# Updating both triangles of a block inverse by products, instead of one by products and one by transposes

## The reference, cut to what matters

```
m = jnp.where(strict, jnp.einsum('bhnrd,bhnsd->bhnrs', kb, k) * decay, 0.0)
t_mat = m + jnp.eye(c, dtype=m.dtype)
w = lax.linalg.triangular_solve(t_mat, kb * jnp.exp(G)[..., None],
                                left_side=True, lower=True, unit_diagonal=True)
u = lax.linalg.triangular_solve(t_mat, v * beta[..., None],
                                left_side=True, lower=True, unit_diagonal=True)
```

## Time and profile before

| what | value |
|---|---|
| runs before | 1982.77, 1983.9 and 1984.44 us, median 1983.9 us |
| profiled execution | 1982.77 us, its span 1981.0 us |
| PE busy | 1905.2 us, 96% of the span |
| DVE, ACT, POOL busy | 997.3, 749.4, 228.9 us |
| mean granted clock of TensorE | 0.985 |
| share of PE in the chain that ended last | 90% |

### The profile page before, as it was taken

How to read it: one execution, slowest core, us unless ns; L and a number is a source line. 1 busy time by engine, 2 the same in 40 slices (tenths; PEclk the granted TensorE clock), 3 DMA queues, 4 the chain that set the end, 5 groups by cost and what they waited for, 6 DMA issues and landing times.

```text
span 1981.0 us, 25408 instructions
## 1 busy us (share of the span) xinstructions
PE 1905.2 (96%) x8897; PEld 1543.1 (78%) x8897; DVE 997.3 (50%) x1467; ACT 749.4 (38%) x1081; POOL 228.9 (12%) x196
## 2 busy tenths in 40 slices
PE   7989978889999999999999999999999999999998
PEld 6778856567788888888878888888776778888887
DVE  5463478754677774344454444433557443434322
ACT  5542543443544443232233323222455443222322
POOL 0051000012111111100021111110000111111100
PEclk9999989899999999999999999999999999999999
DMA  6310210011333333333333333333321123333332
GB/s 188 86 32 1 54 33 22 22 64 54 95 95 95 95 93 97 97 96 98 101 89 96 95 95 95 92 97 98 91 80 43 33 85 96 97 99 99 89 97 72
DMA packets 309219, 161.23 MB, mean 81 GB/s; under 512 B 12688, under 2 KB 306832, under 8 KB 309024
## 3 DMA queue, kind: packets, MB, share of 16 engines
q1 hardware_dynamic: 308080, 157.64, 27.6%
q0 software_dynamic: 640, 2.17, 0.3%
q10 hardware_dynamic: 432, 0.52, 0.1%
HBM read 158.21 MB, written 2.10 MB: 81 GB/s over the span
## 4 chain that ended last, share of the span: by engine, by line
PE 90%; DVE 5%; ACT 2%; issue 2%; DMA 1%; SPq 0%; POOL 0%; DVEq 0%; ACTq 0%; POOLq 0%
PE ps L365 26%; PE ps L367 26%; PE ps L366 26%; PE ps L1404 1%; PE ps L1019 1%; PE ps L1610 1%; PE ps L1419 1%; PE ps L1031 1%; PE ps L1900 1%; PE ps L1901 1%; PE ps L892 1%; PE ps L1395 1%; PE ps L1601 1%; DMA mx<-in_x 0%; PE ps L1239 0%
## 5 line engine op out<-in xcount | busy, mean ns | idle before, releaser
L365 PE MATMUL ps<-xhi,whi 128*128 128x512 f32 x1656 | 661.5, 399 | 10.1 <-DVE xlo L437 6.7
L366 PE MATMUL ps<-xlo,whi 128*128 128x512 f32 x1656 | 646.2, 390 | 0.0
L367 PE MATMUL ps<-xhi,wlo 128*128 128x512 f32 x1656 | 646.1, 390 | 0.0
L352 ACT ACTIVATE whi<-raw 128x1024 fp32r<-128x1024 f32 (+2 forms) x297 | 308.9, 1040 | 716.1 <-PE ps L367 713.5
L360 DVE TENSOR_TENSOR wlo<-raw,whi 128x1024 fp32r<-128x1024 f32 (+2 forms) x297 | 365.8, 1232 | 281.3 <-ACT whi L352 281.2
L365 PEld LDWEIGHTS ps<-xhi,whi 128*128 128x128 f32 x1656 | 312.0, 188 | 82.3 <-issue 5.4
L367 PEld LDWEIGHTS ps<-xhi,wlo 128*128 128x128 f32 x1656 | 311.8, 188 | 66.0
L366 PEld LDWEIGHTS ps<-xlo,whi 128*128 128x128 f32 x1656 | 312.1, 188 | 65.4 <-issue 3.7
L594 DVE TENSOR_TENSOR zS<-ps,rs 128x512 f32<-128x512 f32 x132 | 91.3, 692 | 293.7 <-PE ps L367 284.6
L367 PE MATMUL ps<-h_hi,wlo 128*128 128x512 f32 x528 | 205.4, 389 | 0.0
L365 PE MATMUL ps<-h_hi,whi 128*128 128x512 f32 x528 | 205.4, 389 | 0.0
(11 more groups left out here) (320 smaller groups left out, 1784.1 us busy)
## 6 DMA issues: line engine op xcount, KB each, us to landing
raw<-in_conv_ffn_w SPq DMA_DIRECT2D x52, 512.0 KB, 3.8
raw<-in_mla_ffn_w SPq DMA_DIRECT2D x52, 512.0 KB, 3.8
raw<-in_w_up SPq DMA_DIRECT2D x44, 512.0 KB, 3.7
raw<-in_w_in SPq DMA_DIRECT2D x28, 512.0 KB, 3.8
raw<-in_conv_w_in SPq DMA_DIRECT2D x24, 512.0 KB, 3.7
raw<-in_w_down SPq DMA_DIRECT2D x16, 448.0 KB, 3.6
raw<-in_conv_ffn_w SPq DMA_DIRECT2D x16, 448.0 KB, 3.6
raw<-in_mla_ffn_w SPq DMA_DIRECT2D x16, 448.0 KB, 3.6
```

The costliest lines, as they stand in the source:

```text
L352: a.activation(whi[:, u % PARTS, 0:n], raw[:, u % RAW, 0:n], ACT.Copy).then_inc(hi_split, 1)
L365: t_.matmul(out, wh, xh, start=first, stop=False)
L366: t_.matmul(out, wh, xl, start=False, stop=False)
L367: return t_.matmul(out, wl, xh, start=False, stop=last)
```

## The change

For the levels below 32 the transposes go. In their place PE makes X O X itself, in the columns of X that change (the first half of each pair), with the same 128 x 64 helper, right ahead of its transpose, head by head. DVE now waits for both results of a head, subtracts the first from `X_` and then the second from `XT_`. The next level's Y waits for the first of these. Level 32 is as it was. `credit` shrinks from 40 columns to 8, which moves all later SBUF tiles down by 128 bytes a partition.

```diff
-        credit = sb("credit", [P, 40])
+        credit = sb("credit", [P, 8])
...
-                    pe.wait_ge(*after(f"gdn X1 {h} taken" if b == 2 else f"gdn X{b // 2} {h} taken"))
+                    pe.wait_ge(*after(f"gdn X1 {h} taken" if b == 2 else f"gdn XOX{b // 2} {h} taken"))
                     pe_block_products(pe, f"gdn Y{b} {h}", mx[:, o_tile(b, h), :], mx[:, X_ + h, :])
                 for h in range(4):
                     pe.wait_ge(*after(f"gdn Y{b} {h} taken"))
                     if b > 2:
                         pe.wait_ge(*after(f"gdn XOXT{b // 2} {h} taken"))
+                    if b < 32:
+                        pe_half_products(pe, f"gdn XOX{b} {h}", mx[:, XT_ + h, :], mx[:, OX + h, :], b, False)
                     pe_half_products(pe, f"gdn XOXT{b} {h}", mx[:, OX + h, :], mx[:, XT_ + h, :], b, True)
-                if b < 32:
-                    for h in range(4):
-                        pe_transpose(pe, f"gdn X{b} {h}", mx[:, XT_ + h, :], f"gdn XOXT{b} {h} taken")
...
                 for h in range(4):
+                    dve.wait_ge(*after(f"gdn XOXT{b} {h} full"))
+                    if b < 32:
+                        x, bank = halves(mx[:, X_ + h, :], b, False), full(dve, f"gdn XOX{b} {h}")[:, 0:T // 2]
+                        v.tensor_tensor(x, x, bank.rearrange("p (n b) -> p n b", b=b), ALU.subtract).then_inc(
+                            *step("dve", f"gdn XOX{b} {h} taken"))
                     x, bank = halves(mx[:, XT_ + h, :], b, True), full(dve, f"gdn XOXT{b} {h}")[:, 0:T // 2]
...
-                if b < 32:
-                    for h in range(4):
-                        v.tensor_copy(halves(mx[:, X_ + h, :], b, False),
-                                      halves(full(dve, f"gdn X{b} {h}"), b, False)).then_inc(
-                                          *step("dve", f"gdn X{b} {h} taken"))
```

## The result

| | before | after |
|---|---|---|
| median | 1983.61 us (4 runs, 1982.77 to 1984.44) | 2002.72 us (4 runs, 2001.36 to 2004.43) |
| ratio | | 1.0097, 95% interval 1.008 to 1.0114 |
| profiled execution, its span | 1982.77, 1981.0 us | 2003.55, 2001.7 us |

The kernel became slower, as forecast, but by 19.1 us and not by 7.1; 2002.7 lies outside the range of 1987.8 to 1994.0. The forecast was wrong in size, and the greater part of the loss is at a place where it had booked nothing.

A forecast was written before the change was run, and what follows sets the result against it. The prediction took PE's issue to bound the kernel: 14.08 us of half products added less 7.00 us of transposes removed, all else 0, took the median from 1983.9 to 1991.0 us, range 1987.8 to 1994.0.

The forecast's parts named there:

- The step that failed: Layout behind credit: later tiles moving by 128 bytes cost 0, since no operand changes shape or stride.
- the half-product batch: 16 added matmuls at each of levels 2 to 16: 3.52 us a level, bounded by 1.75 and 3.57 us.
- What bounds the stage: In the inverse, PE sets the pace: busy 40.60 of 40.60 us, 8.84 us a level.
- The price of a record: On PE in the inverse: an fp32 half product costs two records, 0.220 us, a transpose one, 0.109 us.
- The rival by which 64 columns cost half: In the inverse, half products paid by columns: 1.79 us per 16, +0.2 us in all, 1984.1 us; chance 0.04.
- The sum for the products: Levels 2 to 16: 14.08 us of half products added, 7.00 us of transposes removed, +7.08 us.
- The waits: In the changed levels, added waits stay hidden, cost 0; rival with an exposed wait: 1995.1 us, chance 0.04.
- Absorption: Behind the stage, 0 of the delay absorbed; rival with more than 3.1 us absorbed: about 1987 us, chance 0.02.
- The clock: Behind the inverse, shifted clock falls save 60% of 20.4 us lost, giving 1978.8 us; chance 0.01.
- The rivals as a set: Half products paid by columns (0.04), an exposed wait (0.04), partial absorption behind the stage (0.02), faster through the clock (0.01).
- PE pays for every added record: Main case, in the inverse: the added PE work costs its full length, +7.1 us, within 1988.0 to 1993.5; chance 0.89.

The follow-up runs named there:

- a_credit40: The kernel after the change with credit back at 40 columns, so only the new products remain; 1991.3 us, ratio 1.004 against the kernel before.
- b_front32: The kernel before with an unused tile of 32 columns ahead of xT, moving all tiles 128 bytes higher; 1982.91 us, ratio 0.9997.
- b_credit8: The kernel before with only credit cut from 40 to 8 columns, later tiles 128 bytes lower; 1994.26 us, ratio 1.0054.
- b_credit72: The kernel before with credit at 72 columns, only the later tiles 128 bytes higher; 1994.84 us, ratio 1.0054.

## Why the prediction was wrong

**The step that failed** is the one that booked the shrunken tile: "The 128 bytes by which later tiles move cost 0 as well: no operand changes its shape or stride." It measures +10.8 us (1.0054, interval 1.0037 to 1.007), more than the rest of the change. The reason given was not enough: shapes and strides stayed, and the matmuls on `h_hi` and `h_lo` still start 233.3 ns apart in place of 226.7. The other unseen cost, the half-product batch, had been bounded from both sides; this edit had not been, although it moves the operands of about a quarter of the weight matmuls (1584 of 6552).

**What bounds the stage** held. PE is without a pause in the new stretch at the full clock, and its list sets the time.

**The price of a record** held: 64 records in 7.09 us, 0.111 each, against 0.110. The rival by which 64 columns cost half is refuted: 7.09 us, and a_credit40, the products alone, is 7.9 us slower. Its 1991.3 us are what the forecast of 1991.0 for both halves priced.

**The sum for the products** was 7.08 and measures 7.5 us in the profile: 4 x (7.09 - 3.52 - 1.75) = 7.3, and Y takes 3.63 in place of 3.57 at four levels, 0.2. The runs say 7.9 (5.2 to 10.7 by the interval). The first w product, forecast 7.1 us later, starts 7.8 us later in a_credit40 (187.54 against 179.75), 0.3 of it from ahead of the stage.

**The waits** cost 0, as worked out. PE waited in the stage for nothing, DVE waited for PE 16 times before L1125, and POOL's masks came in time.

**Absorption** was not quite 0 in the profiles. In a_credit40 the first w product starts 7.8 us later and the span ends 6.9 us later (1987.9 against 1981.0). The difference arises at L808 (434.89 against 428.33, 6.6 us later), where the wait of 1.1 us on the transfer of x is gone. The prediction said that this transfer moves too, and it is issued 7.6 us later (426.83 against 419.25); but it lands sooner behind its issue, in a median of 5.0 us in place of 5.4. Profiles of kernels that differ in the layout alone have this wait (b_front32, 1.0 us) or lack it (b_credit8, b_credit72), so it can't be put down to the delay. It is too small to show in the medians.

**The clock**, the rival on the faster side, did nothing for the change that can be seen: the mean granted clock is 0.985 in both profiles. Single falls lie at other places and move parts of the profiled executions by up to 2 us, as at 84, 429 and 1003.6 us above.

**The rivals as a set** were too narrow. Two lay inside the stage and two in the waits and the clock behind it; none was a price of the new layout. The chance of 0.93 for slower was right, and the 0.89 for "PE pays for every added record" was given to an account that left out over half of the diff's cost (10.8 of 18.7 us).

## What to carry to other kernels

A tile that changes its size moves every tile allocated after it, and that alone can cost more than the edit one is looking at: when a diff changes any allocation, compare the mean ns of matmul groups whose lines were not edited, and put the old layout back before judging the rest. Where PE streams 512 columns in fp32r and loads new weights for every matmul, as here, try to keep the two operands a multiple of 256 bytes apart in a partition; for other forms measure first, since the transposes of this kernel did not mind. And on a PE that never pauses count records, not columns, up to 128 columns with a load of 128 each: an fp32 half product is two records, a transpose one.

## What the runs showed of the hardware

For fp32r matmuls of 128 x 512 that follow one another without a pause, a start comes every 226.7 ns when moving and stationary operands lie a multiple of 256 bytes apart in a partition of SBUF, and every 233.3 ns, 2.9% more, at other distances (-128, -64, -32, +32 and +128 bytes from such a place). At 2.4 GHz these are 544 and 560 cycles, worked out from the two means. At +128 and -128 the slow starts are uneven, 229 and 237 ns in turn; at -64 all are 233 or 234. A move of all tiles together by 128 bytes has no effect: 1982.91 against 1983.45 us. With the stationary operand of one pass moved by 128 bytes, the pass beside which it is loaded and the pass that uses it both last longer (396 and 397 against 389 ns). What in the memory or in PE's reads makes it so was not found, and neither was why +64 bytes is mixed (394, 388 and 392 ns).

fp32 matmuls with 64 columns cost as much as ones with 128 where each has a load of 128 stationary columns: 0.111 us a record (7.09 us for 64) against 0.113 (3.63 us for 32). That the load sets this pace fits, but no run changed the load.
